# The row factor of two RMS norms moved behind the product in a two-block transformer layer, and the first loads reordered

## The chip, the cores and the metric

The kernel runs on one core of one Trainium2 chip. The metric is the device time in microseconds (us) of one execution, the median over several runs. The engines are named as the profile names them: PE (TensorE, matmul), DVE (VectorE), ACT (ScalarE), POOL (GpSimd) and SP (SyncE, which here issues nearly all DMAs).

## What is computed

Two blocks run one after the other on X, 256 rows of 2048 numbers. The change touches the first block only:

```
h    = rms_norm(x, g_mix)                 # x * rsqrt(mean(x^2) + eps) * g_mix
proj = h @ w_in                           # 2048 x 9216: q, k, v, u, v_sg, two gates
q, k = rms_norm per head; o = stick-breaking attention(q, k, v)
s    = spatial gating of gelu(u), gelu(v_sg)
x    = x + (sigmoid(gate_a) * (o @ w_oa) + sigmoid(gate_b) * (s @ w_ob)) @ w_out
h2   = rms_norm(x, g_ff)
x    = x + square(relu(h2 @ w_ff1)) @ w_ff2     # 2048 x 8192 x 2048
```

`rsqrt(mean(x^2) + eps)` is one number per row of x, the row factor. The second block (modulated norms, neighbourhood attention, a Fourier and a long-convolution branch, a gated feed-forward) has norms with a shift behind the gain, and is left as it is.

## The kernel before

X is kept transposed in SBUF, 128 partitions by 16 tiles of 256 rows, and is handled in four quarters of four tiles. Every large product has the weights as the stationary operand. Its precision comes from a split: each operand is written as a rounded high part and a low part (the rest), and three products are added, high by high, high by low and low by high. For X these parts are XH and XL (the first two tiles of XH lie apart, in XH_FIRST), for the hidden layer HH and HL, for the weights WH and WL.

Weights come in **chunks** of 1 MB: 512 rows by 512 columns. SP loads chunk after chunk into RAW, a ring of four slots; a slot is refilled when its chunk has been converted. ACT copies half a chunk into WH (L484), DVE subtracts it into WL (L867), PE runs 24 products on that half (L1577). WH and WL hold two chunks, so a half can be converted only when PE has finished the same half of the chunk two before. Four chunks make one group, an accumulation in PSUM over all of X into one of two slots; a group then has to be taken out of its slot (`acc_free`) before the group after the next may start. Chunks are counted through the kernel: 0 to 39 the projections, then the gates, C_OAB, C_OUT1 (16 chunks, the output projection), C_FF1 (4 chunks, the first product of the feed-forward), then steps of 8 chunks, four of w_ff1 and four of w_ff2.

Each engine has its own instruction stream, written out in order, with loops over chunks; what else is to be done is put into these streams at given chunks (`if c == ...`), between conversions. DVE's largest extra work is the modulation product of the second block (L1085, L1219): four or two instructions beside most chunks. There is no planner.

Both norms went through `norm_window`: the first two chunks are converted; PE sums the squares over partitions with a product by ones (`norm_sum`, L1649); ACT takes a logarithm and an exponential (`root`, L504 and L506) for the row factor rt; DVE multiplies X by gain and rt into NT (L953, L907); ACT and DVE split NT into XH and XL (L531, L511, L940, L914); and PE starts the group's chunks quarter by quarter. Before the second of them DVE adds the output projection's last quarter to X (L1142) and squares it (L887). In the feed-forward ACT took relu out of PSUM into FR (L658), DVE squared it into FQ (L1170), ACT copied HH (L664) and DVE made HL (L1174). Beside the first two steps of the feed-forward the norm of the second block's context CX is made.

Of the kernel before, what the change touches and what calls it, by code (L numbers as in the profile page):

```python
# [8 lines left out]
P = 128  # L9
T = 256  # L10
# [69 lines left out]
E_NORM1, E_OAB, E_OUT1, E_NORM2, E_CTX, E_NORM3, E_OUT2, E_NORM4 = range(8)  # L80
WINDOWS = [E_NORM1, E_NORM2, E_NORM3, E_NORM4]
# [51 lines left out]
QUARTERS = [0, 4, 8, 12, 16, 18, 19, 20, 24]  # L133
# [16 lines left out]
def build_program(nc, d, out):  # L150
# [6 lines left out]
    with ExitStack() as ctx:  # L157
# [57 lines left out]
        gb = at("gb", [P, KC, T], AR + 56 * K)  # L215
        lng = at("lng", [P, 1024], AR + 40 * K)
# [15 lines left out]
        FQ = at("FQ", [P, FT, T], AR + 36 * K)  # L232
        GS = at("GS", [P, FT, T], AR + 40 * K)
# [100 lines left out]
        def _(sp):  # L334
# [138 lines left out]
        def _(act):  # L473
# [25 lines left out]
            def root(n, total):  # L499
# [4 lines left out]
                own.did(A(rt[:, 0:T], bank(SUM_BANK[n])[:, 0:T], ACT.Ln, bias=epsc[:, 0:1], scale=1.0 / total))  # L504
                own.settle()
                A(rt[:, 0:T], rt[:, 0:T], ACT.Exp, scale=-0.5).then_inc(sm["norm_rt"], 1)  # L506
# [14 lines left out]
            def norm_window(norm, e, c, shift=None):  # L521
# [33 lines left out]

            A(csig[:, :, :], col("c", 0, 2 * KC).rearrange("p (a k) -> p a k", a=2), ACT.Sigmoid)\
                .then_inc(sm["csig_done"], 1)
            act.wait_ge(sm["eps_set"], 1)
            norm_window(N_IN, E_NORM1, Place(0))

            def project_out(g):

                n = g % 2
                t4 = slice(4 * n, 4 * n + 4)
                c5 = slice(n * NB, (n + 1) * NB)
                c, q = Place(4 * g + 3), Place(g)
                if g < 2:
# [38 lines left out]

            for c in range(4, C_OAB):
# [42 lines left out]
            norm_window(N_FF1, E_NORM2, Place(C_FF1))  # L650


            def relu(c, q, j):

                done(c)
                if j.since(1):
                    act.wait_ge(sm["relu_sq"], j.value())
                A(FR[:, :, :], acc_ws(q.slot), ACT.Relu).then_inc(acc_free[q.slot], 1)  # L658

            def hidden_high(j):  # L660
                act.wait_ge(sm["relu_sq"], j.value(1, 1))
# [16 lines left out]
            def ff1_step(j, beside=None):  # L678
                c, q, _ = ff1_place(j)
                for s in range(STEP1):  # L680
                    high(c.plus(s))
                    if beside == 0 and s == 1:
                        relu(c.plus(-1), Place(Q_FF1), Place(0))
                    if beside == 0 and s == 2:
                        hidden_high(Place(0))
                    if s == 5:
                        relu(c.plus(3), q, j.plus(1))
                    if s == 6:
                        hidden_high(j.plus(1))
# [9 lines left out]
            for s in range(3 * SLOTS):  # L699
                high(c.plus(s))  # L700
                if s == 5:
                    relu(c.plus(3), Place(Q_FF1_TAIL), Place(STEPS1 - 1))
                if s == 6:
                    hidden_high(Place(STEPS1 - 1))
# [150 lines left out]
        def _(dve):  # L855
# [60 lines left out]

            def shifted_low(e, hi, lo, src, shift, n):
# [58 lines left out]
            norm_window(N_IN, E_NORM1, Place(0), lambda k: col("g_mix", k), lambda: None)  # L976
# [86 lines left out]
            def beside_modulation(c):  # L1063
# [5 lines left out]
                if 0 <= a < ADA_GATE and n in ADA_AT:  # L1069
# [3 lines left out]
                    if order == 0:  # L1073
                        dve.wait_ge(sm["csil_done"], 1)
                        dve.wait_ge(x_lo, 4)
# [16 lines left out]
            for c in range(4, C_OAB):  # L1092
                low(Place(c))
                if c == T_LN:
# [56 lines left out]
            for t in range(4 * SLOTS):  # L1151
# [10 lines left out]
            norm_window(N_FF1, E_NORM2, Place(C_FF1), lambda k: col("g_ff", k),  # L1162
                        lambda: residual_squares(C_OUT1, Q_OUT1, 3, residual))


            def relu_squared(q, j):
                dve.wait_ge(acc_free[q.slot], q.turns(2, 1))
                if j.since(1):
                    dve.wait_ge(sm["hid_lo"], j.value())
                tt(FQ[:, :, :], FR[:, :, :], FR[:, :, :], ALU.mult).then_inc(sm["relu_sq"], 1)  # L1170

            def hidden_low(j, before=0):
                dve.wait_ge(sm["hid_hi"], j.value(1, before + 1))
                tt(HL[:, j.base % 2], FQ[:, :, :], HH[:, j.base % 2].bitcast(f32), ALU.subtract)\  # L1174
# [51 lines left out]
            def ff1_step(j, beside=None):  # L1226
                c, q, a = ff1_place(j)
                for s in range(STEP1):
# [3 lines left out]
                    if beside == 0 and s == 1:  # L1232
                        relu_squared(Place(Q_FF1), Place(0))
                    if s == 2:
                        hidden_low(j)
                    if s == 5:
                        relu_squared(q, j.plus(1))
# [20 lines left out]
            for s in range(3 * SLOTS):  # L1258
# [9 lines left out]
                if s == 5:  # L1268
                    relu_squared(q, Place(STEPS1 - 1))
# [291 lines left out]
        def _(pe):  # L1561
# [138 lines left out]
            pe.wait_ge(sm["mats_in"], 16)  # L1700
            norm_sum(N_IN, NT)
            for c in range(C_OAB):
                if T_SGU <= c < T_SGU + 8 and (c - T_SGU) % 2 == 0:
# [7 lines left out]
                wide(Place(c), Place(g), s, tok if 4 <= g < 8 else ws, E_NORM1 if g == 0 else None)  # L1711
# [16 lines left out]
            norm_sum(N_FF1, NT, [1])  # L1728
# [22 lines left out]
            for s in range(SLOTS):  # L1751
                wide(Place(C_FF1 + s), Place(Q_FF1), s, e=E_NORM2)
# [315 lines left out]
```

## Time and profile before

| | us |
|---|---|
| median of 3 runs | 2666.87 (2664.70 to 2667.51) |
| the profiled execution | 2667.13 |
| its span, first to last instruction | 2665.0 |

| engine | busy us | share of the span |
|---|---|---|
| PE weight load | 2513.4 | 94% |
| DVE | 1898.5 | 71% |
| ACT | 1172.2 | 44% |

The mean granted clock of PE was 0.990 of full speed. Busy times of different engines overlap, and their shares are means over stages with different limits. DMA moved 558 MB at a mean of 209 GB/s.

### The profile page before, as it was taken

The page shows a single profiled execution, that of the slowest core. Times are in us where ns is not written, and L with a number is a line of the kernel's source. Part 1 is how long each engine was busy: PE and PEld are TensorE (multiplying, and loading weights), DVE is VectorE, ACT ScalarE, POOL GpSimd, SP SyncE. Part 2 cuts the span into 40 slices and gives each one's busy share as a digit, 9 for nine tenths or more (in the row PEclk, how much of TensorE's full clock was granted, in tenths as well). Part 3 has the DMA queues.
Part 4 walks back from the last instruction along what each step waited for, and adds up shares of the span by engine and source line. Part 5 has one row for each costly group of instructions (what it writes and reads, how often), then busy time and mean ns, then how long its engine had stood idle before and what let it go on. Part 6 is the DMA issues. An engine that isn't in the chain of part 4 may idle for free.

```text
span 2665.0 us, 49986 instructions
## 1 busy us (share of the span) xinstructions
PE 2602.8 (98%) x20988; PEld 2513.4 (94%) x20988; DVE 1898.5 (71%) x2411; ACT 1172.2 (44%) x1222; POOL 0.2 (0%) x4
## 2 busy tenths in 40 slices
PE   7999999998999999999999999999899999999998
PEld 6988999998999999999999899948899999999998
DVE  7788887886898888888893236756666666666666
ACT  4766554433544444444442234324354444444443
POOL 0000000000000000000000000000000000000000
PEclk9999999999999999999999999999899999999999
DMA  8665667765788888888772244322455555555553
GB/s 290 215 236 209 227 229 251 248 245 198 260 264 285 282 283 282 283 279 283 266 261 96 95 159 156 130 86 95 158 185 195 190 190 194 197 195 190 191 194 106
DMA packets 282424, 558.23 MB, mean 209 GB/s; under 512 B 10280, under 2 KB 16713, under 8 KB 281929
## 3 DMA queue, kind: packets, MB, share of 16 engines
q1 hardware_dynamic: 282104, 553.60, 60.9%
q8 instruction: 134, 2.20, 0.3%
q10 hardware_dynamic: 144, 2.10, 0.2%
q14 instruction: 42, 0.34, 0.0%
HBM read 553.56 MB, written 2.10 MB: 208 GB/s over the span
## 4 chain that ended last, share of the span: by engine, by line
PE 93%; DVE 4%; issue 1%; ACT 1%; DMA 1%; SPq 0%; DVEq 0%; ACTq 0%
PE PS L1577 79%; PE PS L1587 2%; PE PS L1589 2%; PE PS L1588 2%; DVE WL L867 1%; PE PS L1649 1%; PE PS L1902 1%; PE PS L1913 1%; PE PS L1920 1%; PE PS L1637 0%; PE PS L1736 0%; PE PS L1803 0%; DVE ada1c L1085 0%; DMA RAW<-in_w_in 0%; ACT WH L484 0%
## 5 line engine op out<-in xcount | busy, mean ns | idle before, releaser
L484 ACT ACTIVATE WH<-RAW 128x1024 fp32r<-128x1024 f32 x840 | 888.8, 1061 | 1330.6 <-PE PS L1577 1210.7
L867 DVE TENSOR_TENSOR WL<-RAW,WH 128x1024 fp32r<-128x1024 f32 x840 | 1018.3, 1222 | 628.7 <-ACT WH L484 621.9
L1577 PE MATMUL PS<-XL,WH 128*128 128x256 f32 x4288 | 666.7, 278 | 0.0
L1577 PE MATMUL PS<-XH,WH 128*128 128x256 f32 x3752 | 587.1, 279 | 1.7 <-DVE XL L914 1.5
L1577 PE MATMUL PS<-XH,WL 128*128 128x256 f32 x3752 | 580.1, 277 | 0.0
L1577 PEld LDWEIGHTS PS<-XL,WH 128*128 128x128 f32 x4288 | 571.6, 189 | 0.0
L1577 PEld LDWEIGHTS PS<-XH,WH 128*128 128x128 f32 x3752 | 499.6, 188 | 3.8 <-DVE XL L914 1.7
L1577 PEld LDWEIGHTS PS<-XH,WL 128*128 128x128 f32 x3752 | 496.8, 188 | 0.0
L1577 PE MATMUL PS<-HH,WH 128*128 128x256 f32 x1728 | 268.9, 278 | 1.7 <-DVE X L1180 1.7
L1577 PE MATMUL PS<-HH,WL 128*128 128x256 f32 x1728 | 267.4, 277 | 0.0
L1577 PE MATMUL PS<-HL,WH 128*128 128x256 f32 x1728 | 267.4, 277 | 0.0
L1577 PEld LDWEIGHTS PS<-HH,WH 128*128 128x128 f32 x1728 | 228.9, 188 | 1.9 <-DVE X L1180 1.9
L1577 PEld LDWEIGHTS PS<-HL,WH 128*128 128x128 f32 x1728 | 229.2, 188 | 0.0
L1577 PEld LDWEIGHTS PS<-HH,WL 128*128 128x128 f32 x1728 | 228.9, 188 | 0.0
L1085 DVE SCALAR_TENSOR_TENSOR ada1c<-ada1b,ctmp,ada1c 128x512 f32<-128x512 f32 x240 | 164.3, 745 | 2.1 <-DMA ada1b<-in_ada_w 1.9
L1219 DVE SCALAR_TENSOR_TENSOR adac<-adab,ctmp,adac 128x512 f32<-128x512 f32 x224 | 157.2, 744 | 1.5 <-DMA adab<-in_ada_w 1.3
L1577 PE MATMUL PS<-XH_FIRST,WH 128*128 128x256 f32 x536 | 88.7, 289 | 17.3 <-issue 9.8
L1577 PEld LDWEIGHTS PS<-XH_FIRST,WH 128*128 128x128 f32 x536 | 75.0, 194 | 19.4 <-issue 12.5
L1589 PE MATMUL PS<-WH,XL 128*128 128x512 f32 x224 | 87.8, 392 | 0.0
L1577 PE MATMUL PS<-XH_FIRST,WL 128*128 128x256 f32 x536 | 86.3, 284 | 0.0
L1587 PE MATMUL PS<-WH,XH 128*128 128x512 f32 x196 | 78.5, 400 | 0.0
L1180 DVE TENSOR_TENSOR X<-PS,X 128x1024 f32<-128x1024 f32 x64 | 77.9, 1216 | 0.0
(253 smaller groups left out, 1965.7 us busy)
## 6 DMA issues: line engine op xcount, KB each, us to landing
RAW<-in_w_ff SPq DMA_DIRECT2D x128, 1024.0 KB, 5.6
RAW<-in_w_in SPq DMA_DIRECT2D x112, 1024.0 KB, 5.0
RAW<-in_w_up SPq DMA_DIRECT2D x88, 1024.0 KB, 4.9
adab<-in_ada_w SPq DMA_DIRECT2D x128, 512.0 KB, 4.8
RAW<-in_w_down SPq DMA_DIRECT2D x44, 1024.0 KB, 5.0
ada1b<-in_ada_w SPq DMA_DIRECT2D x64, 512.0 KB, 6.0
RAW<-in_w_out SPq DMA_DIRECT2D x32, 1024.0 KB, 5.1
RAW<-in_w_oa SPq DMA_DIRECT2D x8, 1024.0 KB, 5.3
```

The costliest lines, as they stand in the source:

```text
L484: A(WH[:, c.base % 2, hs], RAW[:, c.base % SLOTS, hs], ACT.Copy).then_inc(hi_done, 1)
L867: tt(WL[:, b, hs], RAW[:, c.base % SLOTS, hs], WH[:, b, hs].bitcast(f32), ALU.subtract)\
L1085: stt(acc, w, x, acc, ALU.mult, ALU.add)
L1180: tt(quarter(X, s), acc_ws(q.slot), quarter(X, s), ALU.add).then_inc(acc_free[q.slot], 1)
L1219: ins = ts(acc, w, x, None, ALU.mult) if n == 0 else stt(acc, w, x, acc, ALU.mult, ALU.add)
L1577: ins = MM(out[:, f, :], w[:, b, kk, f * P:(f + 1) * P], x, start=first and n == 0 and f % 2 == 0, stop=last and n == 2, skip_group_check= ...
L1587: MM(out[:, t, :], h, wh, start=first, stop=False)
L1588: MM(out[:, t, :], h, wl, start=False, stop=False)
L1589: ins = MM(out[:, t, :], l, wh, start=False, stop=last)
L1649: ins = MM(bank(SUM_BANK[norm])[:, 0:T], ones, sq[:, 4 * every[n] + k, :], start=n == 0 and k == 0, stop=n == len(every) - 1 and k == 3)
L1902: ins = MM(bank(n % 2), Ef[:, t, e0:e0 + P], hSD[:, o, 1 if m in (2, 3) else 0, t, :], start=t == 0, stop=t == 1)
L1913: ins = MM(bank(4 + w), Ef[:, t, e0:e0 + P], zt[:, t, :], start=t == 0, stop=t == 1)
```

## The change

For the first norm, group 0 of the projection (chunks 0 to 3) is now made from X times the gain alone (`gain_high`, `gain_low`), and the row factor is multiplied in when DVE takes it out of PSUM (`first_out`). The sum of squares stands on PE ahead of chunk 2, and the root follows. Groups 1 and on use XH and XL of the normed X as before, which are made quarter by quarter over those of the gain (`normed`, `normed_high`, `normed_low`) beside chunks 2 to 6; the fourth quarter of the normed X lies in a buffer of its own (NS).

For the second norm, X times the gain is split into XH and XL beside the output projection, a quarter at a time, and stays there for all 16 products with w_ff1. The row factor (rt_ff1, the second half of rt) is put in behind: `relu_scaled` on DVE takes the larger of 0 and the product out of PSUM and multiplies by the factor, and ACT squares that twice, into HH and into FQ. The second part of the sum of squares stands ahead of the third chunk of C_FF1.

The loads begin with cols and the first quarter of X; the other quarters and mats follow behind weight chunks 0 and 1. The core of the diff:

```diff
-            for n in range(4):
+            def load_x(n):
                 sp.dma_start(X[:, 4 * n:4 * n + 4, :], xq[n]).then_inc(x_in[n], 16)
-            sp.dma_start(mats[:, :, :], d["mats"]).then_inc(sm["mats_in"], 16)
+
             sp.dma_start(cols[:, :], d["cols"]).then_inc(sm["cols_in"], 16)
+            load_x(0)
...
                 load(Place(c), src)
+                if c == 0:
+                    load_x(1)
+                if c == 1:
+                    load_x(2)
+                    sp.dma_start(mats[:, :, :], d["mats"]).then_inc(sm["mats_in"], 16)
+                    load_x(3)
...
+            def gain_high(name, n):
+
+                for k in range(4 * n, 4 * n + 4):
+                    ins = A(tile_of(XH, k), X[:, k, :], ACT.Copy, scale=col(name, k))
+                ins.then_inc(x_hi, 1)
...
+            for n in range(2):
+                act.wait_ge(x_in[n], 16)
+                gain_high("g_mix", n)
+                high(Place(n))
             A(csig[:, :, :], col("c", 0, 2 * KC).rearrange("p (a k) -> p a k", a=2), ACT.Sigmoid)\
                 .then_inc(sm["csig_done"], 1)
+            for n in range(2, 4):
+                act.wait_ge(x_in[n], 16)
+                gain_high("g_mix", n)
+            high(Place(2))
+            high(Place(3))
             act.wait_ge(sm["eps_set"], 1)
-            norm_window(N_IN, E_NORM1, Place(0))
+            root(N_IN, D)
...
             for c in range(4, C_OAB):
                 high(Place(c))
-                if c % 4 == 1 and c < C_GATE + 2:
+                if c < 7:
+                    normed_high(c - 3)
+                if c % 4 == 1 and 5 < c < C_GATE + 2:
                     project_out((c - 5) // 4)
...
+                if c in (C_OUT1 + 6, C_OUT1 + 10, C_OUT1 + 14):
+                    residual_high((c - C_OUT1 - 6) // 4)
+            high(Place(C_FF1))
+            high(Place(C_FF1 + 1))
+            residual_high(3)
+            high(Place(C_FF1 + 2))
+            high(Place(C_FF1 + 3))
+            act.wait_ge(sm["q_done"], 8)
+            root(N_FF1, D, rt_ff1)
+
+            def hidden_high(q, j):
+                act.wait_ge(acc_free[q.slot], q.turns(2, 1))
                 if j.since(1):
                     act.wait_ge(sm["hid_lo"], j.value())
-                A(HH[:, j.base % 2], FQ[:, :, :], ACT.Copy).then_inc(sm["hid_hi"], 1)
+                A(HH[:, j.base % 2], FR[:, :, :], ACT.Square).then_inc(sm["hid_hi"], 1)
+                A(FQ[:, :, :], FR[:, :, :], ACT.Square).then_inc(sm["relu_sq"], 1)
...
+            def gain_low(name, e, n):
+
+                dve.wait_ge(x_hi, 4 * e + n + 1)
+                for k in range(4 * n, 4 * n + 4):
+                    ins = stt(tile_of(XL, k), X[:, k, :], col(name, k), tile_of(XH, k).bitcast(f32),
+                              ALU.mult, ALU.subtract)
+                ins.then_inc(x_lo, 1)
...
             for n in range(4):
                 dve.wait_ge(x_in[n], 16)
+                if n == 0:
+                    dve.wait_ge(sm["cols_in"], 16)
+                gain_low("g_mix", E_GAIN1, n)
+                if n < 2:
+                    low(Place(n))
                 squares(NT, X, n, n == 3)
                 if n in (1, 2):
                     add_squares(NT, n, n == 2)
+            low(Place(2))
+            low(Place(3))
...
+            inverse_root(N_IN)
+            normed(0)
+            normed(1)
+            normed_low(0)
...
             for c in range(4, C_OAB):
                 low(Place(c))
+                if c < 7:
+                    if c < 6:
+                        normed(c - 2)
+                    normed_low(c - 3)
+                if c == 4:
+                    first_out()
...
+                if t in (7, 11, 15):
+                    gain_low("g_ff", E_GAIN2, (t - 7) // 4)
                 beside_modulation(C_OUT1 + t)
+            low(Place(C_FF1))
+            low_half(Place(C_FF1 + 1), 0)
+            residual_squares(C_OUT1, Q_OUT1, 3, residual)
+            low_half(Place(C_FF1 + 1), 1)
+            gain_low("g_ff", E_GAIN2, 3)
+            low(Place(C_FF1 + 2))
+            low(Place(C_FF1 + 3))
+            inverse_root(N_FF1)
+
+            def relu_scaled(c, q, j):
+
+                done(c)
                 if j.since(1):
-                    dve.wait_ge(sm["hid_lo"], j.value())
-                tt(FQ[:, :, :], FR[:, :, :], FR[:, :, :], ALU.mult).then_inc(sm["relu_sq"], 1)
+                    dve.wait_ge(sm["relu_sq"], j.value())
+                    dve.wait_ge(sm["hid_hi"], j.value())
+                stt(FR[:, :, :], acc_ws(q.slot), 0.0, rt_ff1.unsqueeze(1).to_broadcast([P, FT, T]), ALU.max, ALU.mult)\
+                    .then_inc(acc_free[q.slot], 1)
...
             for c in range(C_OAB):
+                if c == 2:
+                    pe.wait_ge(sm["mats_in"], 16)
+                    norm_sum(N_IN, NT)
...
             for s in range(SLOTS):
-                wide(Place(C_FF1 + s), Place(Q_FF1), s, e=E_NORM2)
+                if s == 2:
+                    norm_sum(N_FF1, NT, [1])
+                wide(Place(C_FF1 + s), Place(Q_FF1), s, e=E_GAIN2)
```

New functions that it calls:

```python
            def normed(n):                       # DVE
                for k in range(4 * n, 4 * n + 4):
                    ins = stt(NT[:, k, :] if n < 3 else NS[:, k - 12, :], X[:, k, :], col("g_mix", k), rt[:, 0:T],
                              ALU.mult, ALU.mult)
                ins.then_inc(sm["norm_h"], 1)

            def first_out():                     # DVE
                done(Place(3))
                tt(quarter(qT, 0), acc_ws(0), rt[:, 0:T].unsqueeze(1).to_broadcast([P, FT, T]), ALU.mult)\
                    .then_inc(acc_free[0], 1)
```

## Rows read from the trace of the kernel before

**Rows 1.** The page, part 1: busy time, share of the span, instructions of each engine.

```profile
PE 2602.8 (98%) x20988; PEld 2513.4 (94%) x20988; DVE 1898.5 (71%) x2411; ACT 1172.2 (44%) x1222; POOL 0.2 (0%) x4
```

**Rows 2.** Waits of PE to 700 us: engine line waited for, total us, times, longest.

```profile
PE PS L1649 <- DVE NT L894: 11.5, 1, 11.5
PE PS L1577 <- DVE XL L940: 6.2, 1, 6.2
```

**Rows 3.** The chain of waits, first 90 us: start us, us, what.

```profile
24.11 40.02 PE PS L1577 x336
64.13 1.72 PE PS L1670 x4
65.85 22.60 PE PS L1577 x192
```

**Rows 4.** The same chain around the second norm.

```profile
651.17 1.23 DVE X L1142
...
655.70 4.65 issue
660.35 62.69 PE PS L1577 x528
```

**Rows 5.** Stretches: length; busy us of PE, PEld, DVE, ACT, POOL; clock, DMA share, GB/s.

```profile
8.00:10.00 2.00, 0.00 (x0) 0.00 (x0) 1.97 (x2) 0.00 (x0) 0.00 (x0) 1.00 1.07 370
...
27.00:28.00 1.00, 1.00 (x9) 1.00 (x8) 1.00 (x4) 0.51 (x1) 0.00 (x0) 0.83 0.00 0
...
662.00:663.00 1.00, 1.00 (x6) 1.00 (x6) 1.00 (x4) 0.35 (x1) 0.00 (x0) 0.50 1.05 391
...
665.00:666.00 1.00, 1.00 (x8) 1.00 (x8) 0.34 (x1) 0.12 (x1) 0.00 (x0) 0.69 0.00 0
...
724.00:765.00 41.00, 39.32 (x342) 39.04 (x341) 38.29 (x57) 26.55 (x37) 0.00 (x0) 1.00 0.79 254
```

**Rows 6.** DMA issues: KB of each, median us from issue to landing.

```profile
RAW<-in_w_in SPq DMA_DIRECT2D x112, 1024.0 KB, 5.0
...
X<-in_x SPq DMA_DIRECT2D x4, 512.0 KB, 5.5
...
mats<-in_mats SPq DMA_DIRECT2D x1, 256.0 KB, 7.2
cols<-in_cols SPq DMA_DIRECT2D x1, 237.5 KB, 7.2
```

**Rows 7.** Timeline of ACT: start, length, what, and its idle time before.

```profile
13.57 2.00 ACT L484 ACTIVATE WH<-RAW 128x1024 fp32r<-128x1024 f32 x2 [2.54 <-DMA RAW<-in_w_in]
...
684.88 1.06 ACT L484 ACTIVATE WH<-RAW 128x1024 fp32r<-128x1024 f32 x1 [1.60 <-PE PS L1577]
...
1933.31 1.69 ACT L518 ACTIVATE XH<-NT,mod 128x256 fp32r<-128x256 f32 x4
```

**Rows 8.** Groups by form: count, busy us, mean ns, idle before.

```profile
L504 ACT ACT_TABLE_LOAD x9 | 11.5, 1283 | 0.2
...
L672 ACT ACTIVATE CSQ<-CX 128x1024 f32<-128x1024 f32 x4 | 4.2, 1045 | 0.0
...
L907 DVE SCALAR_TENSOR_TENSOR NT<-X,cols,rt 128x256 f32<-128x256 f32 x40 | 16.3, 478 | 4.5 <-ACT rt L506 4.5
...
L1121 DVE TENSOR_TENSOR ga<-PS,ga 128x1024 f32<-128x1024 f32 x4 | 4.9, 1217 | 0.0
```

**Rows 9.** Timeline of DVE beside the projections and the output projection.

```profile
51.92 2.74 DVE L1085 SCALAR_TENSOR_TENSOR ada1c<-ada1b,ctmp,ada1c 128x512 f32<-128x512 f32 x4 [1.87 <-DMA ada1b<-in_ada_w]
54.58 2.35 DVE L867 TENSOR_TENSOR WL<-RAW,WH 128x1024 fp32r<-128x1024 f32 x2
...
600.75 1.23 DVE L867 TENSOR_TENSOR WL<-RAW,WH 128x1024 fp32r<-128x1024 f32 x1 [1.66 <-ACT WH L484]
```

**Rows 10.** One step of the feed-forward loop on DVE and ACT.

```profile
1115.65 1.22 DVE L1170 TENSOR_TENSOR FQ<-FR 128x1024 f32<-128x1024 f32 x1
...
1118.85 1.07 ACT L484 ACTIVATE WH<-RAW 128x1024 fp32r<-128x1024 f32 x1 [1.66 <-PE PS L1577]
```

More of the change, by code:

```diff
@@ L78 @@
 T_BIAS, T_ATT2 = 17, 21
-E_NORM1, E_OAB, E_OUT1, E_NORM2, E_CTX, E_NORM3, E_OUT2, E_NORM4 = range(8)
-WINDOWS = [E_NORM1, E_NORM2, E_NORM3, E_NORM4]
+E_GAIN1, E_NORM1, E_OAB, E_OUT1, E_GAIN2, E_CTX, E_NORM3, E_OUT2, E_NORM4 = range(9)
+WINDOWS = [E_NORM3, E_NORM4]
 def column_bank(a):
@@ L215, in build_program @@
         gb = at("gb", [P, KC, T], AR + 56 * K)
+        NS = at("NS", [P, FT, T], AR + 56 * K)
         lng = at("lng", [P, 1024], AR + 40 * K)
@@ L232, in build_program @@
         FQ = at("FQ", [P, FT, T], AR + 36 * K)
+        rt_ff1 = rt[:, T:2 * T]
         GS = at("GS", [P, FT, T], AR + 40 * K)
@@ L497, in evac, with root @@
                 A(dst, acc_ws(q.slot) if ws else acc_as(q.slot), fn, scale=scale).then_inc(acc_free[q.slot], 1)
-            def root(n, total):
+            def root(n, total, dst=rt[:, 0:T]):
                 act.wait_ge(sm["norm_sum"], n + 1)
@@ L503, in root @@
                     act.wait_ge(sm["norm_h"], QUARTERS[n])
-                own.did(A(rt[:, 0:T], bank(SUM_BANK[n])[:, 0:T], ACT.Ln, bias=epsc[:, 0:1], scale=1.0 / total))
+                own.did(A(dst, bank(SUM_BANK[n])[:, 0:T], ACT.Ln, bias=epsc[:, 0:1], scale=1.0 / total))
                 own.settle()
-                A(rt[:, 0:T], rt[:, 0:T], ACT.Exp, scale=-0.5).then_inc(sm["norm_rt"], 1)
+                A(dst, dst, ACT.Exp, scale=-0.5).then_inc(sm["norm_rt"], 1)
+            def gain_high(name, n):
+                for k in range(4 * n, 4 * n + 4):
+                    ins = A(tile_of(XH, k), X[:, k, :], ACT.Copy, scale=col(name, k))
+                ins.then_inc(x_hi, 1)
             def split_high(dst, src, n):
@@ L566, in project_out @@
                 c, q = Place(4 * g + 3), Place(g)
-                if g < 2:
+                if g == 1:
                     evac(c, q, qT[:, t4, :], ACT.Copy)
@@ L649, in _ @@
                     split_high(MH, ga[:, 12:16, :], 3)
[L650 to L661, printed above, removed]
+                if c in (C_OUT1 + 6, C_OUT1 + 10, C_OUT1 + 14):
[8 more added lines that the diff above has]
+            def hidden_high(q, j):
+                act.wait_ge(acc_free[q.slot], q.turns(2, 1))
                 if j.since(1):
                     act.wait_ge(sm["hid_lo"], j.value())
-                A(HH[:, j.base % 2], FQ[:, :, :], ACT.Copy).then_inc(sm["hid_hi"], 1)
+                A(HH[:, j.base % 2], FR[:, :, :], ACT.Square).then_inc(sm["hid_hi"], 1)
+                A(FQ[:, :, :], FR[:, :, :], ACT.Square).then_inc(sm["relu_sq"], 1)
             def context_norm(step, s):
@@ L681, in ff1_step @@
                     high(c.plus(s))
-                    if beside == 0 and s == 1:
-                        relu(c.plus(-1), Place(Q_FF1), Place(0))
                     if beside == 0 and s == 2:
-                        hidden_high(Place(0))
-                    if s == 5:
-                        relu(c.plus(3), q, j.plus(1))
+                        hidden_high(Place(Q_FF1), Place(0))
                     if s == 6:
-                        hidden_high(j.plus(1))
+                        hidden_high(q, j.plus(1))
                     if beside is not None:
@@ L975, in _, with normed_low @@
                 .then_inc(sm["csil_done"], 1)
-            norm_window(N_IN, E_NORM1, Place(0), lambda k: col("g_mix", k), lambda: None)
+            def normed(n):
+                for k in range(4 * n, 4 * n + 4):
+                    ins = stt(NT[:, k, :] if n < 3 else NS[:, k - 12, :], X[:, k, :], col("g_mix", k), rt[:, 0:T],
+                              ALU.mult, ALU.mult)
+                ins.then_inc(sm["norm_h"], 1)
+            def normed_low(n):
+                dve.wait_ge(pe_half, 2 * n + 2)
+                split_low(E_NORM1, XH, XL, quarter(NT, n) if n < 3 else NS[:, :, :], n)
+            def first_out():
[6 more added lines that the diff above has]
+            normed_low(0)
             def layer_norm(t, step):
@@ L1160, in _ @@
                     add_squares(NT, (t - 6) // 4, t == 14)
+                if t in (7, 11, 15):
+                    gain_low("g_ff", E_GAIN2, (t - 7) // 4)
                 beside_modulation(C_OUT1 + t)
[L1162 to L1167, printed above, removed]
+            low(Place(C_FF1))
[8 more added lines that the diff above has]
+                done(c)
                 if j.since(1):
-                    dve.wait_ge(sm["hid_lo"], j.value())
-                tt(FQ[:, :, :], FR[:, :, :], FR[:, :, :], ALU.mult).then_inc(sm["relu_sq"], 1)
+                    dve.wait_ge(sm["relu_sq"], j.value())
+                    dve.wait_ge(sm["hid_hi"], j.value())
+                stt(FR[:, :, :], acc_ws(q.slot), 0.0, rt_ff1.unsqueeze(1).to_broadcast([P, FT, T]), ALU.max, ALU.mult)\
+                    .then_inc(acc_free[q.slot], 1)
             def hidden_low(j, before=0):
                 dve.wait_ge(sm["hid_hi"], j.value(1, before + 1))
+                if not before:
+                    dve.wait_ge(sm["relu_sq"], j.value(1, 1))
                 tt(HL[:, j.base % 2], FQ[:, :, :], HH[:, j.base % 2].bitcast(f32), ALU.subtract)\
@@ L1710, in _ @@
                 g, s = divmod(c, SLOTS)
-                wide(Place(c), Place(g), s, tok if 4 <= g < 8 else ws, E_NORM1 if g == 0 else None)
+                wide(Place(c), Place(g), s, tok if 4 <= g < 8 else ws,
+                     {0: E_GAIN1, 1: E_NORM1}.get(g))
             for n in range(4):
```

24 lines of the change are left out of this document (13 added, 11 removed).

## The prediction

> **What bounds the kernel now.** I read the page first. TensorE is busy for 98% of the span [rows 1], so a step can pay only where TensorE waits, where its clock is down, or where it does less work; this change does no less work on it. The waits by engine then name the places [rows 2]: the two longest, 11.5 and 6.2 us, both lie ahead of the first product, and nothing of their size follows but 4.7 us ahead of the first feed-forward product [rows 4]. Third, the chain of waits around each. In the first [rows 3] the reader sees 24.1 us pass before the first product: loads, two conversions of RAW, the logarithm and exponential of the row factor, the scaling, the split. In the second [rows 4] the last product of the output projection ends at 651.15, then come residual, squares, sum and root, and the next product starts at 660.35: 9.2 us with a 2.0 us sum in them. Last, the clock by stretch [rows 5]: in both places TensorE starts at half clock (1.2 GHz) after its idle time; from the means of 0.83 and 0.69 it is back at 2.4 GHz at about 27.3 and 665.6, that is 3.2 and 5.3 us after the product started. A chunk (48 products) takes about 5.46 us at full clock.
>
> **Part 1, the first window.** Where the old order has X, mats and cols ahead of the first weight chunk, the new one has cols and a quarter of X: 2048 + 256 + 237.5 + 1024 KB become 237.5 + 512 + 1024 KB [rows 6]. That is 1.84 MB less, at the 370 GB/s of 8 to 10 us [rows 5] 5.0 us. ScalarE took that chunk up at 13.57 [rows 7], so now at 8.6. One half converted (1.06), its rest taken (1.22) [rows 8]: TensorE starts at about 11.0 instead of 24.11. X times the weight is split meanwhile: four ScalarE instructions of 256 columns (1.69 for four, [rows 7]) and four VectorE ones (1.6).
>
> From there VectorE decides, since it holds a queue without a gap. From 9.7 until the first half of chunk 6 is split it has: 13 half-chunks at a spacing of 1.14 (two take 2.35 with their tail, [rows 9]), six squares or sums of 1.25, three gain splits and four normed quarters of 1.6, three splits of these (3.6 in all), first_out 1.14, ctmp 0.2, and the modulation of chunks 4 and 5, 2.1 and 2.7 [rows 9]. Sum: 14.8 + 7.5 + 11.2 + 3.6 + 1.1 + 0.2 + 4.8 = 43.2, so it ends at 52.9. TensorE by the same steps: chunks 0 and 1 with a cold start end at 23.6 to 25; the sum of squares, now ahead of chunk 2, waits for the fourth quarter's squares until 26.5 and ends at 28.3 (eight instructions 1.73); chunks 2 and 3 end at 39.2. The root runs beside them (28.3 to 31.8), and quarter 0 of the normed X is split by 35.9: no wait at chunk 4. But chunk 5 waits 0.7 for VectorE, and chunk 6, which would start at 50.8, waits for 52.9. It ends at 58.5; with the head sums (1.72) chunk 7 starts at 60.2. Before, it started at 65.85 [rows 3]. The window is worth **5.6 us**; 13 us earlier at the start, of which the sum of squares that now stands in TensorE's stream (3.5, with its wait 4.7) and VectorE's lateness (2.9) take most. After chunk 7 VectorE has 5.0 us or less of work to a chunk and catches up. The clock's restart costs 1.7 (as at 24.1) to 3 us, but the sum waits for VectorE anyway, so it hides. If VectorE's queue costs nothing the window gives 8.4; if it holds 4 us more (0.1 us on each of some 40 instructions), 1.6.
>
> **Part 2, the second window.** Here no product waits for the root any more. XH and XL of quarters 0 to 2 are made under the output projection: 1.69 on ScalarE and 1.6 on VectorE three times. VectorE sits idle for 1.5 us and more ahead of most halves there from 597 on [rows 9]; at chunk 7, the fullest, the added 1.6 moves the next half to 598.8, and TensorE wants it at 602. Cost 0; uncovered it would be 1.6. So chunk C_FF1 starts at 651.15. For chunk C_FF1+1 VectorE has to finish the residual and squares (1.22 + 1.23) and the second half of WL: 654.8, wanted at 656.8. Quarter 3's gain split is done at 656.5, wanted at 669.5. The second part of the sum goes ahead of chunk C_FF1+2. Chain: 651.15 + 5.66 + 5.46 + 1.73 + 5.45 + 5.45 = 674.9. Before, the fourth chunk ended at 684.87, when ScalarE took the half up that it frees [rows 7]. The window is worth **10.0 us**, of which 7.4 is the idle time and 2.6 the clock. The root runs by 667.3 and is first wanted at 677. I see nothing that brings the stall back; bounds 6 (a wait of 4 for a load or a conversion) to 10.3.
>
> The Trainium skill (TensorE: Matmul & The Clock Gate, Terms) puts the penalty of the throttle at the throttled time times one minus the clock's share; by it 5.3 us at 0.50 cost 2.65, and the trace agrees with 2.6. The skill (ScalarE: Activation LUTs, Table sets) also says that one set holds both exponential and logarithm, so that a root should pay one table load. The trace disagrees: 1.28 us of load at the logarithm of all nine roots [rows 8], and as much again at the exponential. By the page the second window would hold 1.3 less to win, and the sum would be 2652.8; the rows decide.
>
> **Part 3, the feed-forward.** Per product, ScalarE's Relu out of PSUM and VectorE's square (1.22, [rows 10]) become, with ScalarE's copy of like size, a VectorE instruction out of PSUM with the factor, and two Squares on ScalarE (1.045 each, and no table load before them, [rows 8]). VectorE: one for one; ScalarE 1.1 more in a step of eight chunks, 44.7 us. The new VectorE form does not exist before; bounds are 1.22 (tensor-tensor out of PSUM, L1121) and 4 × 0.48 = 1.9 (the scalar-tensor-tensor form of 256 columns), and I take 1.22, as the operation is one pass over as many elements [rows 8]. What it moves is the release of the PSUM slot: in the loop from about 1115.4 to 1115.65 + 1.22 = 1116.9, and TensorE wants it as the next chunk ends, at 1118.85 [rows 10]. Spare 2.0: cost 0. In the two steps that hold the context norm VectorE is busy for 38.3 of 41 us [rows 5] and runs late, so TensorE may wait up to 1 us more for the slot there; but VectorE sets the pace in that stretch and gets no more work, so this is absorbed. Bounds 0 to +1.
>
> **The sum.** 2667.13 (profiled execution, span 2665.0) less 5.6 less 10.0 is 2651.5; the median of the runs is 0.3 below the profiled one, which I leave out. Everything behind each window hangs on TensorE's progress, also the stretches where VectorE sets the pace, and the loads run ahead, so both gains are kept to the end.
>
> **Rivals.**
> *A, VectorE keeps up at the start.* Then chunk 7 starts at 57.4 and the total is 2667.1 - 8.4 - 10.0 = 2648.7. For it: durations in a dense queue may overlap a little more. Against it: a queue without a gap over 43 us, each conversion allowed to run only one chunk ahead.
> *B, VectorE holds more.* 4 us more at the start: 2655.5. For it: X in quarters between weight chunks, and semaphore steps that I count at nothing.
> *C, the PSUM slot is freed late in the feed-forward (the slower side).* The slot now hangs on VectorE, with 2.0 us to spare in the loop. If the new instruction took over 3.2 us, as a slow read of a broadcast operand could, TensorE would wait in each of 16 products: at 4.7 us it is 1.5 × 16 = 24 us and 2675. Against it: no VectorE form of 1024 columns in [rows 8] is over 1.9.
> *D, the context load.* 2 MB of CX go into the queue ahead of chunk C_FF1+4 at 651.16, as before, but TensorE is 10 us earlier. At 391 GB/s that chunk lands at 661.7 and is wanted at 666.7; at half the rate it is 4 us late, 2655.5, and with chunks behind it late as well up to 2662. Against it: 391 GB/s in that very stretch [rows 5].
>
> **How the numbers follow.** Forecast 0.62 (own range 2648 to 2656), A 0.13, B 0.12, D 0.08, C 0.05. What can be told from no change is 0.2%, 5.3 us: faster is below 2661.5. Forecast, A, nearly all of B and half of D are faster: 0.89. Half of D and a mild C are the same, 0.07; slower 0.04. For the range I take 2645 (A and a second window at its upper bound) to 2659 (B, and D at its first price).
>
> **What would show it.** First product at 10 to 12 us; VectorE busy without a gap from 10 to 55; head sums at 57 to 60; no wait over 1 us between 640 and 665 on the old scale, no half clock there; a step of the feed-forward loop still at 44.7. It is wrong if chunk 7 starts later than 63, if TensorE waits for loads near C_FF1+4, or if the loop step grows.

## The result and the profile after

The changed kernel takes 2649.11 us (median of 4 runs, 2648.40 to 2650.77) against 2667.19 us (2664.70 to 2667.51) of the kernel before on the same chip. The ratio is 0.9935, with a 95% interval of 0.9918 to 0.9952: 0.65% faster, where 2651.5 was forecast. The profiled execution took 2650.77 us, with a span of 2648.9 and a mean granted clock of 0.994; it is 16.4 us under the profiled execution of before, and its span 16.1 under. All that follows is read from these two spans. One of the five runs of second_only, an experiment below, took 3267.93 us at a mean granted clock of 0.75, and its numbers there are those of the other four.

Page of the changed kernel, part 1, as in [rows 1]: engine, busy us, share, instructions.

```profile
PE 2597.3 (98%) x20988; PEld 2509.4 (95%) x20988; DVE 1900.0 (72%) x2423; ACT 1179.5 (45%) x1249; POOL 0.2 (0%) x4
```

TensorE has as many instructions as before and is busy 5.5 us less: it does the same work at a higher clock or a quicker pace. VectorE has 12 instructions more and ScalarE 27. Then TensorE's waits before 690 us, which answer to [rows 2]: total us, times, longest.

```profile
PE PS L1668 <- DVE WL L903: 15.0, 4, 11.7
PE PS L1728 <- DVE ada1c L1157: 1.6, 1, 1.6
PE PS L1740 <- DVE NT L923: 0.7, 1, 0.7
PE PS L1778 <- DVE lk L1118: 0.5, 1, 0.5
```

The waits of 11.5 and 6.2 us have become one of 11.7 ahead of the first product and three small ones (3.3 together), all for WL, VectorE's subtraction. The chain of waits shows where (start us, us, what); it answers to [rows 3].

```profile
27.10 2.01 PE PS L1740 x8
29.18 1.28 ACT L513
...
45.33 2.35 DVE WL L903 x2
47.68 1.58 DVE NS L1031 x4
49.26 1.14 DVE XL L950
50.40 1.40 DVE ada1c L1157 x3
...
52.97 1.23 DVE WL L903
54.20 0.14 issue
54.34 5.89 PE PS L1668 x48
60.23 1.72 PE PS L1761 x4
61.94 21.90 PE PS L1668 x192
```

Between the sum (L1740) and chunk 6, which begins at 54.34, the chain runs through VectorE for nearly the whole way, and chunk 7 starts at 61.94 where it started at 65.85 before: 3.9 us gained. The second window, same columns, answers to [rows 4]:

```profile
622.47 16.43 PE PS L1668 x144
638.90 1.73 PE PS L1740 x8
640.63 16.45 PE PS L1668 x144
657.09 1.73 PE PS L1740 x8
658.81 16.22 PE PS L1668 x142
```

Here nothing but TensorE is left. The output projection ends inside the x144 (48 products, 5.47 us, after 640.63, so at 646.10), two chunks with w_ff1 follow at once, and the second part of the sum stands at 657.09. In stretches (length; busy us of PE, PEld, DVE, ACT, POOL; clock, DMA share, GB/s), the line that answers to 665:666 of [rows 5] is

```profile
659.00:662.00 3.00, 3.00 (x29) 3.00 (x28) 0.44 (x1) 2.96 (x4) 0.00 (x0) 1.00 1.05 386
```

with the granted clock at 1.00 (2.4 GHz) instead of 0.50 to 0.69. ScalarE takes up the half that the fourth chunk frees (start, length, what, idle before; [rows 7] had it at 684.88):

```profile
669.75 1.06 ACT L493 ACTIVATE WH<-RAW 128x1024 fp32r<-128x1024 f32 x1 [1.59 <-PE PS L1668]
```

So the fourth chunk is 15.1 us early: from the end of the output projection to there, 33.73 us before and 23.65 now, 10.1 us gained. The span's 16.1 us are then 3.9 (first window), 0.3 (by 280 us), 0.8 (626 to 651), 10.1 (second window) and 1.0 at the last feed-forward's norm near 1900 us, where sum and first chunk took 3.78 + 7.48 us before and 1.99 + 8.18 now. TensorE's code at the other three places is the same before and after.

### The profile page after: what moved, and what is told of

Read it like the earlier page. It is cut to its first block, busy times and chain, and to the rows that moved or that the text cites. A ratio compares the mean times of both kernels' runs of the same rounds, so it can differ in the third digit from the quotient of the medians.

```text
span 2648.9 us, 50027 instructions
## 1 busy us (share of the span) xinstructions
PE 2597.3 (98%) x20988; PEld 2509.4 (95%) x20988; DVE 1900.0 (72%) x2423; ACT 1179.5 (45%) x1249; POOL 0.2 (0%) x4
## 4 chain that ended last, share of the span: by engine, by line
PE 93%; DVE 4%; issue 1%; ACT 1%; DMA 1%; SPq 0%; DVEq 0%; ACTq 0%
PE PS L1668 79%; PE PS L1678 3%; PE PS L1680 2%; PE PS L1679 2%; DVE WL L903 1%; PE PS L1740 1%; PE PS L1996 1%; PE PS L2007 1%; PE PS L2014 1%; PE PS L1728 1%; PE PS L1828 0%; PE PS L1897 0%; DMA RAW<-in_w_in 0%; DVE ada1c L1157 0%; PE PS L1932 0%
## 5 line engine op out<-in xcount | busy, mean ns | idle before, releaser
L1157 DVE SCALAR_TENSOR_TENSOR ada1c<-ada1b,ctmp,ada1c 128x512 f32<-128x512 f32 x240 | 164.4, 745 | 0.2
L1668 PE MATMUL PS<-XH_FIRST,WH 128*128 128x256 f32 x536 | 87.8, 287 | 18.0 <-DVE WL L903 11.7
```

The lines of the kernel that those rows point to most:

```text
L1157: stt(acc, w, x, acc, ALU.mult, ALU.add)
L1668: ins = MM(out[:, f, :], w[:, b, kk, f * P:(f + 1) * P], x, start=first and n == 0 and f % 2 == 0, stop=last and n == 2, skip_group_check= ...
```

## The experiments

All are edits of the changed kernel, if not said otherwise. Ratios are to runs of the kernel before on the same chip (medians of 2665.35 to 2667.19); they can differ by up to 0.001 from the quotient of the medians. The last column is read from the profiled execution.

| | median us (range) | ratio (95%) | chunk 7 at, us |
|---|---|---|---|
| changed kernel | 2649.11 (2648.40 to 2650.77) | 0.9935 (0.9918 to 0.9952) | 61.94 |
| first_only | 2662.37 (2660.17 to 2663.42) | 0.9984 (0.9974 to 0.9993) | 61.50 |
| second_only | 2656.19 (2654.01 to 2657.34) | 0.9959 (0.9943 to 0.9975) | 67.57 |
| old_loads | 2654.80 (2651.19 to 2656.84) | 0.9952 (0.9935 to 0.9968) | 66.24 |
| ada_short | 2647.07 (2646.57 to 2649.32) | 0.9929 (0.9912 to 0.9945) | 59.14 |
| act_squares | 2648.59 (2646.72 to 2651.30) | 0.9938 (0.9921 to 0.9955) | 59.19 |
| ada_later | 2647.92 (2642.57 to 2648.92) | 0.9928 (0.9911 to 0.9944) | 57.88 |
| both | 2645.80 (2641.80 to 2646.82) | 0.9923 (0.9906 to 0.9939) | 57.59 |
| release_1 | 2653.88 (2652.10 to 2655.80) | 0.9957 (0.9940 to 0.9974) | 61.55 |
| release_2 | 2736.28 (2727.93 to 2739.61) | 1.0253 (1.0232 to 1.0274) | 61.59 |
| warm_before | 2693.74 (2689.86 to 2696.66) | 1.0108 (1.0091 to 1.0125) | 66.70 |
| shift_only | 2698.17 (2689.71 to 2703.06) | 1.0114 (1.0088 to 1.0139) | 65.92 |
| warm_four | 2663.49 (2661.16 to 2667.17) | 0.9991 (0.9981 to 1.0001) | 66.48 |

**The two halves of the change.** first_only is the change without its part on the second norm, second_only that part alone.

```diff
 first_only
-            high(Place(C_FF1))
...
-            root(N_FF1, D, rt_ff1)
+            norm_window(N_FF1, E_NORM2, Place(C_FF1))
 second_only
-                if c == 2:
-                    pe.wait_ge(sm["mats_in"], 16)
-                    norm_sum(N_IN, NT)
+            norm_window(N_IN, E_NORM1, Place(0))
```

> The change at the first norm and the loads alone; the second norm and the feed-forward as before. Theory (two windows that add up): chunk 7 starts at 61.9 as in the changed kernel (65.9 before), the product of the feed-forward waits 9.2 us again as before, total 4 us under the kernel before, 2663. Rival (the second window holds the whole gain and the first is given back later): within 1 us of the kernel before.

> The change at the second norm and the feed-forward alone; first norm and loads as before. Theory: chunk 7 starts at 65.9, no wait ahead of the feed-forward, the fourth chunk of it ends 10.1 us earlier than before, total 2657. Rival (the two parts need each other, or the rest of the gain, some 2 us beyond 3.9 and 10.1, belongs to the second): 2655 or less.

first_only starts chunk 7 at 61.50 and then has the old stall at the second window, in its chain of waits:

```profile
648.65 1.99 PE PS L1731 x8
650.64 4.65 issue
655.29 62.98 PE PS L1659 x528
```

second_only has none; with its own lines it is the chain of the changed kernel again:

```profile
646.46 16.45 PE PS L1609 x144
662.91 1.73 PE PS L1681 x8
```

Its output projection ends at 651.93 and its fourth chunk, 10.94 us after 664.64, at 675.58: 23.65 us, 10.1 less than before. Both totals are within 1 us of what was expected, and each window keeps its gain without the other. The medians gain 3.8 and 10.0 us, 13.8 together, where the whole change gains 18.1; the intervals of the ratios are too wide (0.17 points, 4.5 us, to either side for two of the three) to say whether the rest is real. And second_only, whose first window has the old code, starts chunk 7 at 67.57 us, 1.7 later than before: its first 336 products took 41.99 us where [rows 3] has 40.02. Two things differ in its trace. Its granted clock is back at 1.00 at about 28.7 us instead of 27.3, so it starts with 4.8 us at half clock instead of 3.2, which costs some 0.8 us. And its products then keep a pace of 0.47 us for four all the way, where most of those of the kernel before follow in 0.45.

**The loads.**

```diff
+            for n in range(4):
+                load_x(n)
+            sp.dma_start(mats[:, :, :], d["mats"]).then_inc(sm["mats_in"], 16)
             sp.dma_start(cols[:, :], d["cols"]).then_inc(sm["cols_in"], 16)
-            load_x(0)
...
-                if c == 0:
-                    load_x(1)
...
```

> The changed kernel with X, mats and cols loaded ahead of the first weight chunk again. Theory (VectorE's queue decides the first window, and it begins when the first chunk and cols have landed): the first weight chunk lands at 13.6 instead of 9.3, so the first half of WL is ready 4 us later; but X is there earlier and its gain splits and squares no longer wait, so chunk 7 starts 2 to 4 us later than 61.9, total 2651 to 2653. Rival (TensorE's own stream decides, loads early enough anyway): chunk 7 within 0.5 us of 61.9.

The first product comes at 16.01 instead of 11.73, and all of the 4.3 us reaches chunk 7, a little more than the 2 to 4 expected. It starts at 66.24, no earlier than in the kernel before: in the first window the new order of norm and product brings nothing without the new order of the loads. What the loads bring without the rest was not run. The median, 2654.80, lies above the 2651 to 2653 expected.

**Who holds chunks 5 and 6.** Three ways to take work off VectorE there. ada_short cuts six of the first eight modulation instructions (L1156 and L1157) from 512 to 8 columns and so leaves that part of the computation out.

```diff
+                        if order < 2 and (n or m >= 2):
+                            acc, w = acc[:, 0:8], w[:, 0:8]
```

> The changed kernel; of the modulation product beside chunks 4 and 5 six of the eight instructions are cut from 512 to 8 columns (that part of the computation is left out), so VectorE has 3.6 us less in its queue ahead of chunk 6. Theory (VectorE's queue holds TensorE at chunks 5 and 6): the waits of 0.7 and 1.8 us there vanish and chunk 7 starts 2.5 us earlier, at 59.4. Rival (the wait is for the split of the normed X or for the root, the queue is only busy): chunk 7 stays within 0.5 us of 61.9.

act_squares has ScalarE square the first three quarters of X, and takes a logarithm that nobody needs ahead of the root, so that its table is loaded early:

```diff
+            def square(n):
+                A(NT[:, 4 * n:4 * n + 4, :], X[:, 4 * n:4 * n + 4, :], ACT.Square).then_inc(sm["sq_act"], 1)
...
+            A(lnst[:, 15:16], epsc[:, 0:1], ACT.Ln)
             root(N_IN, D)
...
-                squares(NT, X, n, n == 3)
+                if n == 3:
+                    squares(NT, X, n, True)
                 if n in (1, 2):
+                    dve.wait_ge(sm["sq_act"], n + 1)
```

> The changed kernel with the squares of the first three quarters of X moved from VectorE to ScalarE, and a throw-away logarithm ahead of the first root, so that its table is loaded before the sum is there. VectorE's queue loses 3.7 us ahead of the root, the root ends 1.3 us sooner. Theory: the next gap at VectorE (1.0 us at the root) goes, chunk 6 starts 2 to 2.5 us earlier, chunk 7 at about 59.5, total 2647. Rival (ScalarE becomes the one that is waited for in the first 30 us): chunk 7 later than 61.

ada_later starts the first group of pieces two chunks later:

```diff
+ADA_AT0 = [2, 3, 4, 6, 7, 8, 9, 10]
...
-                if 0 <= a < ADA_GATE and n in ADA_AT:
-                    n = ADA_AT.index(n)
+                at = ADA_AT if a else ADA_AT0
+                if 0 <= a < ADA_GATE and n in at:
+                    n = at.index(n)
```

> The changed kernel with one edit: the first group of modulation pieces on VectorE starts two chunks later, so that chunks 4 and 5 carry none and the pieces of later chunks are denser. In the changed kernel PE waits 0.7 us at chunk 5 and 1.75 us at chunk 6 for VectorE's weight copies. Theory: these waits come from VectorE's backlog, so they go, chunk 7 starts near 59.4 us instead of 61.9, and the total is about 2647. Rival: the same VectorE work, only postponed, makes the copies of chunks 8 to 14 late and gives it back: 2649 or more, with waits for VectorE in PE's rows after 62 us.

Each starts chunk 7 earlier by 2.75 to 4.1 us, with TensorE's instructions unchanged, so the queue of VectorE was what held it. In act_squares, where squares and table are changed together, the 1.0 us in which VectorE stands idle at the root is gone too. In ada_short TensorE's waits for WL from 12 to 62 us, 2.5 us beside the first, are gone. ada_later's chain goes from the sum to the head sums through TensorE alone:

```profile
26.84 1.99 PE PS L1743 x8
28.83 27.33 PE PS L1671 x240
56.16 1.72 PE PS L1764 x4
57.88 22.60 PE PS L1671 x192
```

The 240 products of chunks 2 to 6 took 27.33 us here, 5.47 to a chunk; in ada_short the same 240, with no wait between them either, took 28.26. So about 0.9 of the 1.3 us between these two is the pace of the products and not VectorE's queue. Nothing is given back later: TensorE's waits to 690 us are three for WL (12.4 in all, 11.5 of them ahead of the first product), the 1.6 and 0.5 of the changed kernel, and 0.4 for its 0.7.

> The changed kernel with two edits together: the squares of the first norm on ScalarE, and the modulation pieces two chunks later. Theory: each takes work off VectorE in the first 60 us; squares on ScalarE alone left chunk 7 at 59.19 us. If a wait for VectorE is still in that, chunk 7 starts near 57.9 and the total is about 2645, some 4 us under the changed kernel. Rival: PE is already bound by its own products after the first edit, and the second adds nothing: chunk 7 at 59.2, total about 2648.

act_squares and ada_later together start chunk 7 at 57.59, and its span is 2643.4, 5.5 under the changed kernel's. Its median is 3.3 us lower, and the ranges of the runs don't overlap; the intervals of the two ratios do, and the two kernels were not timed beside each other. It is the fastest version here; between ada_later and both the runs do not decide.

**Where the slot is released.** In the loop `relu_scaled` is put behind the modulation pieces of its chunk (release_1), or a whole chunk later (release_2).

```diff
 release_1
-                    if s == 5:
-                        relu_scaled(c.plus(3), q, j.plus(1))
                     if s == 1 and beside is None:
...
+                    if s == 5:
+                        relu_scaled(c.plus(3), q, j.plus(1))
 release_2
                     low(c.plus(s))
+                    if s == 6:
+                        relu_scaled(c.plus(3), q, j.plus(1))
...
-                    if s == 5:
-                        relu_scaled(c.plus(3), q, j.plus(1))
```

> The changed kernel with relu_scaled moved behind the modulation instructions of the same chunk, so that in the feed-forward loop the PSUM slot is freed 1.3 us later. Theory (spare of 2.0 us): TensorE waits nowhere in the loop, a step stays at 44.7, total within 1 us of the changed kernel. Rival (spare is smaller, semaphores and PSUM reads eat it): up to 1.3 us in each of 14 steps, up to 2667.

> The changed kernel with relu_scaled moved behind the conversion of the next chunk, so that in the loop the slot is freed about 5.4 us later. Theory (spare of 2.0 us, then one for one): TensorE waits 3.4 us in each step, 48.1 instead of 44.7, in 15 steps some 50 us, total 2695 to 2702. Rival (VectorE makes the time good, the slot is not what TensorE waits for): under 10 us more.

TensorE's waits from 690 to 1400 us, first in the changed kernel (its only one for FR, beside 1.8 us for X and 1.3 for the squares), then in release_1, then in release_2:

```profile
PE PS L1668 <- DVE FR L1258: 0.8, 1, 0.8
```

```profile
PE PS L1668 <- DVE FR L1258: 4.3, 2, 3.7
```

```profile
PE PS L1668 <- DVE FR L1258: 52.9, 14, 6.0
```

release_1 has none in the loop either, so of the 2 us to spare the 1.3 that it uses up are there. Its 4.3 us lie in the two steps with the context norm, and 707.25 to 1295.85 took 2.2 us more than the 586.4 of the changed kernel. That missed the expected 1 us. Its median is 4.8 above the changed kernel's, but the spans are 1.4 apart and the intervals of the two ratios overlap, so no more than the 2.2 is shown. release_2 waits 3.8 us in a step (3.4 expected), and pays for it in a way that was not expected: 

```profile
1008.31 1.23 DVE FR L1258
1009.54 0.12 issue
1009.65 13.70 PE PS L1668 x96
1023.36 0.79 PE PS L1828 x8
```

The 96 products behind such a wait took 13.70 us instead of 10.9. TensorE stands idle from 1006.05; its granted clock falls within the wait (mean of 0.62 over 1008 to 1009 us), is 0.50 (1.2 GHz) until 1015, and is back at 1.00 at 1016. The mean of 1000 to 1200 us is 0.93, where the changed kernel has 1.00. Fourteen times 2.8 are 39 us on top of 53 of waits: the span is 88.9 longer, and the median of 2736.28 far above the 2695 to 2702 expected.

**The clock's share by itself.** In the kernel before, nine products of 512 columns that nobody needs are put into the 4.65 us of idle time ahead of chunk C_FF1.

```diff
+            for n in range(9):
+                MM(bank(5)[:, 0:T], ones, mats[:, 0:2, :], start=True, stop=True)
```

> The kernel before, with nine products by ones (their result unused) between the second part of the second norm's sum and the first feed-forward product, 3.9 us of work inside TensorE's idle 4.65 us. Theory (10.0 us at the second window are 7.4 of idle time and 2.6 of the clock): the idle time shrinks to under 1 us without the next product starting later, that product's chunk takes 5.5 to 5.7 instead of 8.2, total 2 to 2.6 under the kernel before, 2664. Rival (the slow first chunk is not for the idle time ahead of it): chunk still 7.5 to 8.2, total within 0.5 of before.

Locally the theory held: chunk C_FF1 started at full clock, and the 528 products took 60.31 us instead of the 62.69 of [rows 4]. Yet the median rose by 27.5 us, where a fall by 2 was expected, and the span by 22.8: ten steps of the feed-forward loop, whose code is the same, took 472.5 us instead of 447.3. Two kernels tell the reasons apart: nine products of one column (the same instructions, hardly any work: the trace has 18 matmuls and 18 weight loads more, as in warm_before), and four of 512 (8 and 8 more).

```diff
 shift_only
+            for n in range(9):
+                MM(bank(5)[:, 0:1], ones, mats[:, 0, 0:1], start=True, stop=True)
 warm_four
+            for n in range(4):
+                MM(bank(5), ones, mats[:, :, :], start=True, stop=True)
```

> The kernel before, with nine products of one column each (no work to speak of) put where the experiment warm_before had nine products of 512 columns: PE's instructions behind them lie at the same distance from the start as there. Theory: the 21 us that warm_before lost in the FF1 loop come from where the loop's instructions lie and how they are fetched, so this kernel loses them too: 2687 to 2694, with some 179 packets in the queue that fetches instructions against 134, and waits named issue at L1577. Rival: the added work itself did it (the clock, heat, a shifted phase), then this kernel is within 1 us of the kernel before, 2666 to 2668.

> The kernel before, with four products of 512 columns (about 3.5 us) in the idle time of PE ahead of the second norm's sum, instead of nine. Theory: the clock gained by them is the same 2.4 us as in warm_before (the products behind them at full clock from the start), and with fewer added instructions the FF1 loop does not stall: total about 2664. Rival: any added instruction shifts the loop into the stall, and the total is 2685 or more.

shift_only loses 33 us (2698.17, above the 2687 to 2694 expected) with 1.9 us of work added, and its ten steps take 482.9. The page's part 3 (queue, packets, MB, share), first of warm_four, which is as the kernel before and the changed one, then of shift_only:

```profile
q8 instruction: 134, 2.20, 0.3%
```

```profile
q8 instruction: 179, 2.93, 0.4%
```

TensorE in shift_only, where its first stall lies (start, length, what, and the idle time before), and VectorE there:

```profile
867.16 0.63 PE L1577 MATMUL PS<-HL,WH 128*128 128x256 f32 x4
867.63 0.63 PE L1577 MATMUL PS<-HH,WL 128*128 128x256 f32 x4
871.59 1.22 PE L1577 MATMUL PS<-XH_FIRST,WH 128*128 128x256 f32 x4 [3.32 <-DVE WL L867]
```

```profile
861.75 2.41 DVE L867 TENSOR_TENSOR WL<-RAW,WH 128x1024 fp32r<-128x1024 f32 x2
866.66 1.23 DVE L867 TENSOR_TENSOR WL<-RAW,WH 128x1024 fp32r<-128x1024 f32 x1 [0.57 <-ACT WH L484]
```

TensorE begins here a step's first chunk with w_ff1. WH and WL hold two chunks, so the two halves of the row at 861.75, done at 864.16, are this chunk's, and the half at 866.66, done at 867.89, is already for the chunk after it. TensorE was through with the chunk ahead at 868.28, and yet it starts at 871.59. A stall of this kind stands at 871.59, 967.45 and so on, once in two steps (steps of 44.7, one of 46.1, and of 51.0 to 52.4 us by turns), and two steps are one turn of the program's loop; the slower products behind it cost the rest. With 45 packets more in the queue for instructions, the reading is that TensorE waited for its own instructions: the loop now lies so that part of it is fetched anew in each turn. That the added work doesn't do it is shown. That the place of the loop does, and by a fetch, is inferred from the packets, the turn of the loop and the releaser that was long done; no run moved the loop by another means. warm_four has neither, and keeps the gain: 660.08 to 720.39 is again 60.31 us for the 528 products, 2.38 less. The Trainium skill (TensorE: Matmul & The Clock Gate, Terms) puts the price of a throttled stretch at its length times one minus the clock's share; by that, as an estimate, 5.3 us at 0.50 come to 2.65; the trace agrees roughly, with 2.38. At 1306.77 us it is 2.65 ahead of before, at 1602 still 1.4, and at 1764, behind products of the Fourier branch (L1840) that took 9.80 us instead of 8.83, nothing. At the end 0.7 was left in the span, and the ratio's interval includes 1.

## Why the prediction was right, and where not

*Part 2, the second window: right, 10.1 for 10.0.* The chain without any wait, the clock at 1.00, the sum ahead of the third chunk, chunk C_FF1+1 not late for residual and squares: all as worked out, and second_only shows it alone. warm_before and warm_four confirm that 2.4 of it were clock (2.6 forecast).

*Part 1, the first window: 3.9 for 5.6; the mechanism right, the term mis-sized.* VectorE's queue decides, as forecast, and ada_short, act_squares and ada_later show it. Its work was well counted: from 10.36 to 54.20 less 1.0 idle are 42.8 us for the 43.2 of the prediction. What was off is around it. The first chunk was taken up at 9.27 for 8.6, and the queue began 0.7 late. ScalarE in the changed kernel, start, length, what, idle before:

```profile
5.22 1.28 ACT L520 ACT_TABLE_LOAD   x1 [5.22 <-DMA X<-in_x]
...
9.27 2.00 ACT L493 ACTIVATE WH<-RAW 128x1024 fp32r<-128x1024 f32 x2 [1.05 <-DMA RAW<-in_w_in]
```

And the step "busy without a gap" failed: at the root VectorE is idle for 1.0 us.

```profile
26.97 4.62 DVE L903 TENSOR_TENSOR WL<-RAW,WH 128x1024 fp32r<-128x1024 f32 x4
31.51 0.18 DVE L1025 TENSOR_TENSOR ctmp<-cols,csig 128x32 f32<-128x32 f32 x1
32.71 3.26 DVE L1031 SCALAR_TENSOR_TENSOR NT<-X,cols,rt 128x256 f32<-128x256 f32 x8 [1.02 <-ACT rt L515]
```

From the last squares the way through sum and root is 5.6 us (27.05 to 32.68), and the four halves and ctmp laid beside it are only 4.7. ScalarE, idle for 3.4 us before, loads the logarithm's table only when the sum is there (29.18). With 0.3 for chunk 6 (5.89 for the 5.6 forecast) and 0.1 from the last half of WL to its first product these make 2.1; less the 0.4 us of work that was counted too much, that is the 1.7.

*Part 3, the feed-forward: right.* The unknown VectorE form took what the nearest row gave (690 to 1400 us):

```profile
L1258 DVE SCALAR_TENSOR_TENSOR FR<-PS,rt 128x1024 f32<-128x1024 f32 x15 | 18.3, 1217 | 0.0
```

The loop step stayed at 43.95 + 0.79 us, and the one wait of 0.8 in a context step was absorbed: chunks of the loop start 15.15 us earlier on both sides of it.

*The rivals.* A names 2648.7, within 0.4 of the result, and is still refuted: chunk 7 is at 61.94, not 57.4. Chunk 7 starts where A puts it in ada_later and both, at 57.88 and 57.59. B's 4 us on VectorE were not there. C's mechanism exists, with a higher price than I gave it: release_2 paid 6.4 us in a step, 3.8 of wait and 2.8 of clock less what overlaps, where I counted the wait alone. D did not appear: no wait for a load stands in TensorE's rows to 690 us.

*The total.* 1.7 us short in the first window, 2.1 more at places where the change takes no wait away (0.3, 0.8 and 1.0), and the median 1.7 under the profiled execution, where before it was 0.3: the forecast was 2.4 too high, and that it came so close is in part chance.

Open is why the same products have two pitches. In the first window four products follow in 0.453 or in 0.471 us, 5.46 or 5.66 to a chunk; the 480 of the output projection took 56.78 us in the changed kernel, 56.77 in both and 54.66 in act_squares, with the next 144 at 16.43, 16.44 and 17.07, and no row names a cause. It was not tried.

## What to carry to other kernels

Taking a norm's root off the way of the first product pays in full where the other engines have spare time (10.1 us, idle time and clock together), and only as far as the next queue allows where they don't (3.9): count that queue's work and also the chain that runs beside each of its waits. A wait of TensorE can cost more than its length, 2.8 us of slower clock behind one of 3.8 us here, so look at the granted clock behind it before a later release is priced. And before a small edit of TensorE's stream is judged by its time, compare the packets of the instruction queue: 36 added instructions (18 matmuls, 18 weight loads) went with 25 and 36 us more in ten steps of a loop elsewhere.

## What was not expected of the hardware

- Instructions added far ahead of a loop: 134 packets of instructions and a step of 44.7 us, or 179 and every second step 3.7 to 7.6 us longer. The second sum of the second norm, just ahead of the added products, took 3.56 us in warm_before and 3.39 in shift_only, where it takes 2.00 in the kernel before; the 3.78 us of the last feed-forward's sum in the kernel before look alike, but no run tells why.
- The profile's granted clock reads 1.00 from 12 to 15 us in the changed kernel, while groups of four products follow each other in 0.85 us, as at 0.50 in the kernel before, and only from 15.3 on in 0.58 and 0.47. By their pace the first products ran at half speed all the same.

```profile
12.72 1.05 PE L1668 MATMUL PS<-XL,WH 128*128 128x256 f32 x4
13.58 1.05 PE L1668 MATMUL PS<-XH_FIRST,WL 128*128 128x256 f32 x4
...
15.86 0.63 PE L1668 MATMUL PS<-XH_FIRST,WL 128*128 128x256 f32 x4
16.33 0.52 PE L1668 MATMUL PS<-XH,WH 128*128 128x256 f32 x3
```

- Equal code after an idle time differs by up to 2 us between kernels: 40.02, 40.27, 40.86, 40.95 and 41.99 us for the first 336 products of five kernels that share that code. The granted clock is back at 1.00 at 27.3 us in the first and at 29.3 in the fourth (means of 0.58 over 26.5 to 27.5 us and of 0.60 over 28.5 to 29.5); the third has it back at 27.4 and is slow by the second pace instead, 0.47 us for four products.
